# Running sums of the log decay from a high and a low part in the rounded format

## The chip, the cores and the metric

The kernel runs on one core of one Trainium2 chip. The metric is the device time of one execution in microseconds (us). One execution was also taken by the hardware profiler. The profile's names for the engines are used throughout: PE is TensorE (PEld its weight loads), DVE is VectorE, ACT is ScalarE, POOL is GpSimd, SP is SyncE, which starts the DMA transfers.

## The reference

The reference is two transformer blocks in a row, each on 256 tokens of width 1024. The change lies in the second block, in its gated linear attention (GLA). There a low-rank gate gives each of 4 heads x 64 key channels a log decay per token, which is summed up along the tokens inside chunks of 64:

```python
def gla(q, k, v, g_lr, og, w_gate2, b_gate, norm_o):
    log_a = jax.nn.log_sigmoid((g_lr @ w_gate2 + b_gate).astype(jnp.float32)) / GLA_GATE_TAU   # 16
    gh = heads(log_a, GLA_HEAD_K)
    bcum = jnp.cumsum(chunks(gh), axis=3)                 # running sum in each chunk of 64 tokens
    ...
    def step(state, xs):
        qc, kc, vc, bc = xs
        o_inter = jnp.einsum('bhcd,bhde->bhce', qc * jnp.exp(bc), state)
        diff = bc[:, :, :, None, :] - bc[:, :, None, :, :]
        decay = jnp.exp(jnp.where(causal[:, :, None], diff, -jnp.inf))
        attn = jnp.einsum('bhid,bhjd,bhijd->bhij', qc, kc, decay)
        ...
        b_last = bc[:, :, -1:, :]
        k_dec = kc * jnp.exp(b_last - bc)                 # needs the sum of what comes after a token
```

The rest of the two blocks is large matrix products: input projections, attention, output projections and a gated feed-forward net in each block.

## The kernel before

**Tiling.** Tokens stand on the 128 partitions in two tiles (`TOKS` = 2). Every large product `x @ W` is done in strips of 128 rows of W (one strip is a *unit*, up to 1024 columns wide). W comes from memory by DMA into `weights_raw`, a ring of nine slots (`RING`). Each strip is then split in two by `advance`, which exists on ACT and on DVE: ACT writes the strip rounded to the format `fp32r` (float32r, the rounded format; `weights_high`, line 724), and DVE writes what the rounding left (`weights_low`, line 1574, `raw - high`). PE makes a product in three passes in the rounded format: high x high, high x low, low x high (line 1193), 128x512 each, all accumulating in the PSUM tile `acc`. The small products of the attention parts go to four other PSUM banks, `aux[0]` to `aux[3]`.

**Order.** Nothing is scheduled at run time. The function `timeline` writes one list of steps, and each engine goes through this same list, doing its own part of each step. A weight split is put in front of the first step whose place in the list has passed the strip's due time (`due`, reckoned from where PE needs the strip), so between two steps of an engine there may be one or more splits. `tick` counts up a semaphore, and `at` gives the value to wait for.

**The place of the change.** The GLA gate runs during the projection `gla_qk` (eight strips of 512 columns, line 1193). Its steps are in `timeline`, lines 267 to 269: `decay_logits` after the strip (1, 2), which means token tile 1, strip 2, and `decay_sums` together with `gla_qk_turn` 0 after the strip (1, 7), the last of this projection.

- `decay_logits`: PE makes the gate's logits (line 1436). DVE adds the bias (line 1955) and makes the absolute value (1957). ACT takes exp and ln (986, 989, each with a load of its table). DVE makes the log decay `gl` ("log_decay" in the trace, 128x512 f32: two token tiles of 256 channels; line 1960) and counts up `vec`.
- `decay_sums`: PE waits for `vec` and for the masks `sum_up_to` and `sum_after`, two constant 128x128 matrices of 0 and 1/16 which POOL has made at line 2178 to 2185. It then makes four plain f32 products of 128x128 (line 1447, to `aux[0]`; the log decay is the stationary operand, so these sums come out with channels on the partitions) and two plain f32 products of 128x256 (line 1450, to `aux[1]`). ACT copies the first (`bT`, "decay_sum_T", line 992) and takes exp of the second (`kdec`, "k_decayed", line 994). Each plain f32 product stands in the trace as two records, so there are 8 and 4.
- `gla_qk_turn`: PE transposes the projection (line 1103, 4 per token tile), and goes on with the next projection, `gla_v_og` (line 1193).
- `gla_decay` and what follows on DVE and ACT (1974, 1976, 1007, 1987) work from `bT`.

```python
                elif kind == "decay_sums":            # PE
                    pe.wait_ge(*at("vec", "log_decay"))
                    pe.wait_ge(*at("pool", "sum_masks"))
```

## Time and profile before

| | us |
|---|---|
| time, median of 3 runs | 745.93 (745.63 to 746.54) |
| the profiled execution, its own time | 745.29 |
| span of the profiled execution, first to last instruction | 743.5 |
| PE busy in it | 736.3 (99%), 4082 matmul records |
| PE weight loads busy | 610.1 (82%) |
| DVE busy | 487.1 (66%) |
| ACT busy | 401.9 (54%) |
| POOL busy | 56.5 (8%) |
| mean granted clock of PE | 0.999 |

A matmul record's duration contains the time that the pipeline needs to empty, and the next matmul starts before it ends. What one more matmul costs a busy PE is therefore the distance from its start to the next start, not its duration. In a timeline row the first number is the start, the second the time from that start to the end of the last of the merged records, and "xN" their number. DVE and ACT instructions overlap by some 0.1 us in the same way.

### The profile page before, as it was taken

Reading aid. Unit: us, or ns where it says so; the run is one execution under the profiler, and the core shown is the slowest. Engines: PE = TensorE matmul, PEld = TensorE weight load, DVE = VectorE, ACT = ScalarE, POOL = GpSimd, SP = SyncE. Lnnn points to the kernel's source line nnn. Section 1 sums busy time; section 2 is a strip of 40 time slices with the busy share of each in tenths; the row PEclk is TensorE's granted clock in tenths of the full one; section 3 lists DMA queues with packets and bytes.
Section 4 is the critical chain, followed back from the end, with each engine's and each line's share of the span. In section 5 each row is a group of like instructions: output and inputs, shape, how many; then the busy total and the mean of one; then the engine's idle time right before and its main releaser. Section 6 shows DMA issues by size and latency. Waiting matters only on the chain.

```text
span 743.5 us, 10597 instructions
## 1 busy us (share of the span) xinstructions
PE 736.3 (99%) x4082; PEld 610.1 (82%) x4082; DVE 487.1 (66%) x748; ACT 401.9 (54%) x584; POOL 56.5 (8%) x127
## 2 busy tenths in 40 slices
PE   9999999999999999999999999999999999999996
PEld 7888887888888888888898888888888888888886
DVE  5597777676864756775376877777755576475733
ACT  5656767533653535544368554786435545364422
POOL 1100100000470000000023000200011000000000
PEclk9999999999999999999999999999999999999999
DMA  8856464564755655645476373444465565565541
GB/s 320 274 186 224 129 202 140 169 208 150 240 174 176 211 179 173 225 148 194 135 228 208 111 244 118 145 159 121 143 222 162 180 215 167 184 215 159 193 142 57
DMA packets 57521, 134.36 MB, mean 181 GB/s; under 512 B 7864, under 2 KB 13823, under 8 KB 57471
## 3 DMA queue, kind: packets, MB, share of 16 engines
q1 hardware_dynamic: 56816, 132.16, 54.6%
q10 hardware_dynamic: 654, 1.53, 0.6%
q8 instruction: 32, 0.52, 0.3%
q14 instruction: 19, 0.15, 0.1%
HBM read 132.61 MB, written 1.05 MB: 180 GB/s over the span
## 4 chain that ended last, share of the span: by engine, by line
PE 98%; DMA 1%; ACT 0%; DVE 0%; POOL 0%; ACTq 0%; issue 0%; POOLq 0%
PE acc L1193 88%; PE aux L1103 2%; PE aux L1384 1%; PE aux L1288 1%; PE aux L1411 1%; PE acc L1184 1%; PE aux L1309 1%; PE aux L1470 1%; DMA weights_raw<-in_w_in_dram 1%; PE aux L1375 0%; PE aux L1329 0%; PE acc L1123 0%; PE aux L1350 0%; PE aux L1531 0%; PE aux L1184 0%; PE aux L1502 0%
## 5 line engine op out<-in xcount | busy, mean ns | idle before, releaser
L1193 PE MATMUL acc<-weights_high,h_high 128*128 128x512 f32 (+1 forms) x716 | 227.2, 393 | 0.0
L1574 DVE SCALAR_TENSOR_TENSOR weights_low<-weights_raw,gain_columns,weights_high 128x1024 fp32r<-128x1024 f32 (+3 forms) x189 | 217.6, 1188 | 13.0 <-ACT weights_high L724 12.9
L1193 PE MATMUL acc<-weights_high,h_low 128*128 128x512 f32 (+1 forms) x716 | 222.7, 387 | 0.0
L1193 PE MATMUL acc<-weights_low,h_high 128*128 128x512 f32 (+1 forms) x716 | 222.5, 386 | 0.0
L724 ACT ACTIVATE weights_high<-weights_raw,gain_columns 128x1024 fp32r<-128x1024 f32 (+3 forms) x188 | 194.8, 1074 | 33.4 <-DMA weights_raw<-in_w_up_dram 12.0
L1193 PEld LDWEIGHTS acc<-weights_low,h_high 128*128 128x128 f32 x716 | 133.5, 188 | 27.8 <-DVE weights_low L1574 0.6
L1193 PEld LDWEIGHTS acc<-weights_high,h_low 128*128 128x128 f32 x716 | 133.6, 188 | 27.2
L1193 PEld LDWEIGHTS acc<-weights_high,h_high 128*128 128x128 f32 x716 | 130.4, 188 | 26.0 <-issue 1.0
L1571 DVE TENSOR_TENSOR weights_low<-weights_raw,weights_high 128x1024 fp32r<-128x1024 f32 x68 | 80.7, 1219 | 33.2 <-ACT weights_high L724 33.1
L724 ACT ACTIVATE weights_high<-weights_raw 128x1024 fp32r<-128x1024 f32 x68 | 69.3, 1057 | 48.2 <-DMA weights_raw<-in_ffn_w_down_dram 22.2
L1701 DVE SCALAR_TENSOR_TENSOR silu_tmp<-silu_tmp,acc 128x512 f32<-128x512 f32 (+1 forms) x24 | 15.4, 642 | 74.9 <-ACT silu_tmp L781 74.9
L781 ACT ACTIVATE silu_tmp<-acc,stats 128x512 f32<-128x512 f32 (+1 forms) x24 | 15.7, 654 | 87.2 <-PE acc L1193 87.2
L2130 POOL TENSOR_SCALAR stats<-stats 128x1 f32<-128x1 f32 (+1 forms) x15 | 6.5, 432 | 595.2 <-ACT row L737 278.2
L1193 PE MATMUL acc<-weights_high,y_high 128*128 128x512 f32 (+1 forms) x148 | 45.7, 390 | 0.0
L1193 PE MATMUL acc<-weights_high,y_low 128*128 128x512 f32 (+1 forms) x148 | 45.0, 385 | 0.0
L1193 PE MATMUL acc<-weights_low,y_high 128*128 128x512 f32 (+1 forms) x148 | 45.0, 385 | 0.0
L1193 PEld LDWEIGHTS acc<-weights_high,y_low 128*128 128x128 f32 x148 | 27.7, 188 | 5.4
L1193 PEld LDWEIGHTS acc<-weights_low,y_high 128*128 128x128 f32 x148 | 27.7, 188 | 5.4
L1193 PE MATMUL acc<-weights_high,f_high 128*128 128x512 f32 x102 | 31.5, 390 | 0.0
L1193 PE MATMUL acc<-weights_low,f_high 128*128 128x512 f32 x102 | 31.4, 389 | 0.0
L1193 PE MATMUL acc<-weights_high,f_low 128*128 128x512 f32 x102 | 31.4, 389 | 0.0
L1193 PEld LDWEIGHTS acc<-weights_high,y_high 128*128 128x128 f32 x148 | 27.1, 188 | 5.2 <-issue 0.3
(313 smaller groups left out, 645.2 us busy)
## 6 DMA issues: line engine op xcount, KB each, us to landing
weights_raw<-in_w_in_dram SPq DMA_DIRECT2D x59, 512.0 KB, 4.7
weights_raw<-in_w_gate_dram SPq DMA_DIRECT2D x44, 256.0 KB, 3.3
weights_raw<-in_w_up_dram SPq DMA_DIRECT2D x44, 256.0 KB, 4.1
weights_raw<-in_w_down_dram SPq DMA_DIRECT2D x22, 512.0 KB, 4.5
weights_raw<-in_ffn_w_gate_dram SPq DMA_DIRECT2D x44, 256.0 KB, 3.4
weights_raw<-in_ffn_w_up_dram SPq DMA_DIRECT2D x44, 256.0 KB, 4.2
weights_raw<-in_ffn_w_down_dram SPq DMA_DIRECT2D x22, 512.0 KB, 4.4
weights_raw<-in_w_out_dram SPq DMA_DIRECT2D x16, 512.0 KB, 4.6
```

Of the source, the lines that this page charges most:

```text
L724: nc.scalar.activation(hi[:, u % RING, d:d + w], raw[:, u % RING, d:d + w], ACT.Copy, scale=1.0 if g is None else gcol[:, g:g + 1])\
L781: nc.scalar.activation(fe[:, j % 2, t, 0:w], a0[:, 0:w], ACT.Tanh, scale=stat(("half", (tag, t))))\
L1103: i = nc.tensor.transpose(aux[bank][0:w, n * P:(n + 1) * P], src, ident[:, :])
L1184: i = nc.tensor.matmul(dst, lhs[:, k0, sl], w[:, u % RING, c], start=(alone and n == 0 and kt == first_half), stop=(kt == kts - 1 and n == 2))
L1193: i = nc.tensor.matmul(acc[:, 2 * t + b, 0:width], lhs[:, k0, sl], w[:, u % RING, base + d:base + d + width], start=(kt == 0 and n == 0), ...
L1288: m = nc.tensor.matmul(scores(kind, i, hb), att_q(kind, hb, i, pq), att_k(kind, hb, i, pk), start=(n == 0), stop=(n == 2))
L1309: m = nc.tensor.matmul(scores(kind, i, hb), att_q(kind, hb, i, pq), att_k(kind, hb, i, pk), start=(n == 0), stop=(n == len(passes) - 1))
L1384: m = nc.tensor.matmul(aux[bank][hb * HD:hb * HD + HD, d:d + P], v[:, kt, c:c + HD], probs_block(kind, i, hb, kt), start=(kt == 0), stop=( ...
L1411: i = nc.tensor.transpose(aux[first + g][:, d:d + ROWS], fe[r, int(name[-1]) % 2, t, k * P:(k + 1) * P], ident[r, r])
L1571: i = nc.vector.tensor_tensor(lo[:, u % RING, c], raw[:, u % RING, c], hi[:, u % RING, c].bitcast(F32), ALU.subtract)
L1574: i = nc.vector.scalar_tensor_tensor(lo[:, u % RING, c], raw[:, u % RING, c], gcol[:, g:g + 1], hi[:, u % RING, c].bitcast(F32), ALU.mult, ...
L1701: then(nc.vector.scalar_tensor_tensor(e, e, 1.0, a0[:, 0:w], ALU.add, ALU.mult))
```

## The change

The sums are made from two operands in the rounded format in place of one plain f32 operand. ACT copies `gl` rounded into `gl_parts[0]` ("log_decay_high"), DVE subtracts that from `gl` into `gl_parts[1]` ("log_decay_low"), and POOL copies the two masks into the rounded format. PE then makes each of the six products in two passes, high and low, which accumulate: eight instructions of 128x128 and four of 128x256. PE's wait for the log decay becomes a wait for its low part. A DVE wait behind the log decay is new as well.

```diff
+        sum_masks = [sb(f"{n}_rounded", [P, P], F32R) for n in ("sum_up_to", "sum_after")]
...
+            gl_parts = [sb(f"log_decay_{part}", [P, TOKS, 256], F32R, s) for part in ("high", "low")]
...
                 elif kind == "decay_sums":                                   # ACT
+                    act.wait_ge(*at("vec", "log_decay"))
+                    nc.scalar.activation(gl_parts[0][:, :, :], gl[:, :, :], ACT.Copy).then_inc(*tick("act", "log_decay_high"))
                     act.wait_ge(*at("gla_done", "sums"))
...
                 elif kind == "decay_sums":                                   # PE
-                    pe.wait_ge(*at("vec", "log_decay"))
+                    pe.wait_ge(*at("vec", "log_decay_low"))
                     pe.wait_ge(*at("pool", "sum_masks"))
...
-                            nc.tensor.matmul(aux[0][:, c:c + P], gl[:, t, f * P:(f + 1) * P], upto[:, :],
-                                             start=True, stop=True)
+                            for n, part in enumerate(gl_parts):
+                                nc.tensor.matmul(aux[0][:, c:c + P], part[:, t, f * P:(f + 1) * P], sum_masks[0][:, :],
+                                                 start=(n == 0), stop=(n == 1))
                     for t in range(TOKS):
-                        m = nc.tensor.matmul(aux[1][:, t * 256:t * 256 + 256], after[:, :], gl[:, t, :],
-                                             start=True, stop=True)
+                        for n, part in enumerate(gl_parts):
+                            m = nc.tensor.matmul(aux[1][:, t * 256:t * 256 + 256], sum_masks[1][:, :], part[:, t, :],
+                                                 start=(n == 0), stop=(n == 1))
...
-                                                          ALU.min, ALU.subtract), "vec", "log_decay")
+                                                          ALU.min, ALU.subtract), "vec", "log_decay", True)
+                elif kind == "decay_sums":                                   # DVE
+                    dve.wait_ge(*at("act", "log_decay_high"))
+                    signal(nc.vector.tensor_tensor(gl_parts[1][:, :, :], gl[:, :, :], gl_parts[0][:, :, :].bitcast(F32),
+                                                   ALU.subtract), "vec", "log_decay_low")
...
-                done(g.memset(after[64:128, 0:64], 0.0), "pool", "sum_masks")
+                then(g.memset(after[64:128, 0:64], 0.0))
+                g.tensor_copy(sum_masks[0][:, :], upto[:, :])
+                done(g.tensor_copy(sum_masks[1][:, :], after[:, :]), "pool", "sum_masks")
```

On DVE these instructions stand in a row around the gate of the GLA before the change (L1960 makes the log decay, L1574 is a weight split, L1974 the first use of the sums):

```order
L1955 TENSOR_TENSOR log_decay<-aux,gla_bias_bc 128x256
L1957 SCALAR_TENSOR_TENSOR level_decay<-log_decay 128x512 [waits vec]
L1960 SCALAR_TENSOR_TENSOR log_decay<-log_decay,level_decay 128x512 [waits act]
L1574 SCALAR_TENSOR_TENSOR weights_low<-weights_raw,gain_columns,weights_high 128x1024 [waits high_ready]
L1574 SCALAR_TENSOR_TENSOR weights_low<-weights_raw,gain_columns,weights_high 128x1024 [waits high_ready,mm_done] x2
L1974 TENSOR_TENSOR level_decay<-decay_sum_T 128x8x32 [waits act]
```

And the same place on DVE in the changed kernel, whose lines are numbered some lines higher (L1580 is the weight split):

```order
L1961 TENSOR_TENSOR log_decay<-aux,gla_bias_bc 128x256
L1963 SCALAR_TENSOR_TENSOR level_decay<-log_decay 128x512 [waits vec]
L1966 SCALAR_TENSOR_TENSOR log_decay<-log_decay,level_decay 128x512 [waits act]
L1580 SCALAR_TENSOR_TENSOR weights_low<-weights_raw,gain_columns,weights_high 128x1024 [waits high_ready,vec]
L1580 SCALAR_TENSOR_TENSOR weights_low<-weights_raw,gain_columns,weights_high 128x1024 [waits high_ready,mm_done]
L1970 TENSOR_TENSOR log_decay_low<-log_decay,log_decay_high 128x512 [waits act]
L1580 SCALAR_TENSOR_TENSOR weights_low<-weights_raw,gain_columns,weights_high 128x1024 [waits high_ready,mm_done]
L1984 TENSOR_TENSOR level_decay<-decay_sum_T 128x8x32 [waits act]
```

The subtraction that makes the low part stands behind two of the three weight splits and ahead of the third.

On ACT the same place before the change (L724 is a weight split, L789 the copy of the projection out of PSUM, L992 the copy of the sums):

```order
L989 ACTIVATE level_decay<-level_decay 128x512 [waits act]
L724 ACTIVATE weights_high<-weights_raw,gain_columns 128x1024 [waits gains,raw_loaded1]
L789 ACTIVATE gla_qk<-acc,stats 128x512 [waits rstd,mm_done]
L724 ACTIVATE weights_high<-weights_raw,gain_columns 128x1024 [waits gains,raw_loaded2]
L992 ACTIVATE decay_sum_T<-aux 128x512 [waits gla_done]
```

And in the changed kernel:

```order
L991 ACTIVATE level_decay<-level_decay 128x512 [waits act]
L726 ACTIVATE weights_high<-weights_raw,gain_columns 128x1024 [waits gains,raw_loaded1]
L791 ACTIVATE gla_qk<-acc,stats 128x512 [waits rstd,mm_done]
L726 ACTIVATE weights_high<-weights_raw,gain_columns 128x1024 [waits gains,raw_loaded2]
L994 ACTIVATE log_decay_high<-log_decay 128x512 [waits vec]
L996 ACTIVATE decay_sum_T<-aux 128x512 [waits gla_done]
```

The rounded copy comes behind both weight splits and directly ahead of the copy of the sums.

## Rows read from the trace of the kernel before

**Rows 1.** The page: busy us, share of the span and instructions of each engine.

```profile
PE 736.3 (99%) x4082; PEld 610.1 (82%) x4082; DVE 487.1 (66%) x748; ACT 401.9 (54%) x584; POOL 56.5 (8%) x127
```

**Rows 2.** Waits of PE, whole span: whom for, us in total, times, longest.

```profile
PE aux L1092 <- DVE row L2090: 1.1, 1, 1.1
PE acc L1123 <- ACT weights_high L712: 0.5, 1, 0.5
```

**Rows 3.** Timeline of PE around the sums: start, us to the end, operation, count.

```profile
402.90 0.39 PE L1193 MATMUL acc<-weights_low,h_high 128*128 128x512 f32 x1
403.13 1.05 PE L1447 MATMUL aux<-sum_up_to,log_decay 128*128 128x128 f32 x8
404.02 1.03 PE L1450 MATMUL aux<-log_decay,sum_after 128*128 128x256 f32 x4
404.89 0.60 PE L1103 MATMUL aux<-ident,gla_qk 128*128 128x128 f32 x4
```

**Rows 4.** Timeline of DVE, 397 to 405 us.

```profile
397.54 0.74 DVE L1955 TENSOR_TENSOR log_decay<-aux,gla_bias_bc 128x256 f32<-128x256 f32 x2
398.32 0.69 DVE L1957 SCALAR_TENSOR_TENSOR level_decay<-log_decay 128x512 f32<-128x512 f32 x1
401.66 0.69 DVE L1960 SCALAR_TENSOR_TENSOR log_decay<-log_decay,level_decay 128x512 f32<-128x512 f32 x1 [2.64 <-ACT level_decay L989]
402.27 3.67 DVE L1574 SCALAR_TENSOR_TENSOR weights_low<-weights_raw,gain_columns,weights_high 128x1024 fp32r<-128x1024 f32 x3
```

**Rows 5.** Timeline of ACT, 401 to 406 us.

```profile
401.53 1.14 ACT L724 ACTIVATE weights_high<-weights_raw,gain_columns 128x1024 fp32r<-128x1024 f32 x1
402.57 0.67 ACT L789 ACTIVATE gla_qk<-acc,stats 128x512 f32<-128x512 f32 x1
403.14 1.14 ACT L724 ACTIVATE weights_high<-weights_raw,gain_columns 128x1024 fp32r<-128x1024 f32 x1
405.09 0.60 ACT L992 ACTIVATE decay_sum_T<-aux 128x512 f32<-128x512 f32 x1 [0.81 <-PE aux L1450]
```

**Rows 6.** Groups by line and form, ACT and DVE: count, busy us, mean ns.

```profile
L1036 ACT ACTIVATE k_latent_high<-k_latent_first 96x512 fp32r<-96x512 f32 x2 | 1.1, 622 | 0.0
...
L2058 DVE TENSOR_TENSOR k_latent_low<-k_latent_first,k_latent_high 96x512 fp32r<-96x512 f32 x2 | 1.3, 679 | 0.0
```

**Rows 7.** Timeline of PE: rounded products at 256 columns near the end (15 in a row).

```profile
737.51 0.28 PE L1184 MATMUL aux<-weights_high,f_low 128*128 128x256 f32 x1
737.63 0.28 PE L1184 MATMUL aux<-weights_low,f_high 128*128 128x256 f32 x1
```

**Rows 8.** Weight loads by group: rounded operand, plain operand, transpose; busy us, mean ns.

```profile
L1184 PEld LDWEIGHTS aux<-weights_high,f_high 128*128 128x128 f32 x5 | 1.0, 192 | 0.0
L1447 PEld LDWEIGHTS aux<-sum_up_to,log_decay 128*128 128x128 f32 x8 | 1.0, 191 | 0.1
L1103 PEld LDWEIGHTS aux<-ident,gla_qk 128*128 128x128 f32 x8 | 1.0, 140 | 0.2
```

**Rows 9.** Timelines of ACT and PE around PE's last wait, at 6 us.

```profile
5.80 0.71 ACT L715 ACTIVATE weights_high<-weights_raw,gain_columns 128x512 fp32r<-128x512 f32 x1
...
6.04 1.02 PE L1123 MATMUL acc<-weights_high,h_high 128*128 128x512 f32 x2 [0.46 <-ACT weights_high L712]
6.90 0.62 PE L1123 MATMUL acc<-weights_high,h_low 128*128 128x512 f32 x2
```

**Rows 10.** Timeline of PE in the first microseconds.

```profile
3.31 1.65 PE L1092 MATMUL aux<-row 128*128 128x128 f32 x6
4.75 0.51 PE L1103 MATMUL aux<-ident,x 128*128 128x128 f32 x2
```

**Rows 11.** Stretches behind PE's last product: busy times, granted clock, DMA share, GB/s.

```profile
737.90:742.20 4.30, 0.01 (x1) 0.00 (x0) 1.81 (x5) 0.62 (x1) 0.60 (x1) 1.00 0.24 92
742.30:743.50 1.20, 0.00 (x0) 0.00 (x0) 0.00 (x0) 0.00 (x0) 0.00 (x0) 0.50 0.23 79
```

**Rows 12.** Timeline of POOL: the last instruction on the two masks.

```profile
204.45 0.15 POOL L2185 MEMSET sum_after<- 64x64 f32 x1
```

## The prediction

> **What bounds the kernel now.** I read the page's engine line first: PE is busy for 736.3 of 743.5 us, DVE for 487.1 and ACT for 401.9 [rows 1]. Next the waits of PE over the whole span. There are two, both in the first microseconds: PE starts 1.1 us late, and the later wait ends at 6.04 us [rows 2, 9]. From there to its last product at 737.63 us [rows 7] PE never waits for another engine. The reader is to see two things in this. Time taken out of PE's row of work is gained one for one, and time put into it, as work or as a wait, is lost one for one, because no later wait exists that could swallow it. And a busy second of DVE or ACT costs nothing as long as PE still finds its operands ready. So the change is decided at one place, where PE passes from the projection to the sums. The timelines of PE, DVE and ACT there are read side by side.
>
> **PE before.** The sums start at 403.13, the next step (transposes) at 404.89 [rows 3]. They fill 1.76 us: eight records of 128x128 from 403.13 to 404.02, 0.111 each, and four of 128x256 from 404.02 to 404.89, 0.217 each. There is no gap ahead of them: the last 128x512 record starts at 402.90, 0.23 earlier. The log decay is only just in time for that, since DVE finishes it at 401.66 + 0.69 = 402.35 [rows 4] and PE loads its first sum's weights at about 402.9.
>
> **PE's work after.** Four instructions of 128x256 in the rounded format. Such products stand in the trace at 0.12 from start to start (737.51, 737.63) [rows 7], so 4 x 0.12 = 0.48 in place of 0.87, a gain of 0.39. The eight of 128x128 in the rounded format have no row. Bounds: per column the rounded product costs half of the plain record (0.12 to 0.217 at 256), and a straight line through 0.23 at 512 columns (402.90 to 403.13) [rows 3] and 0.12 at 256 gives 0.065 at 128, so 0.52 for eight. From above, a rounded product that at 128 columns is as dear as a whole plain one (two records) costs 0.22, so 1.78 for eight. Between them stands the weight load. Each of the eight has its own 128x128 load. It lasts 192 ns for a rounded operand and 191 for a plain one, against 140 for a transpose [rows 8]; so the format takes nothing off the load, and consecutive plain 128x128 records with the same load stand 0.111 apart. What a load costs where no product hides it is worked out below, about 0.11. I take 0.115 for each, 0.92 for eight, which is the row of the plain ones and a little: the nearest row by load and columns. PE's work after is 0.92 + 0.48 = 1.40, a gain of 0.36 (bounds 0.76 gain, 0.50 loss).
>
> The Trainium skill has two rules here that point in opposite ways. "FP8 and Floating Point Precision", section "TensorE Precision Notes", has true FP32 as four passes through the array. By it two passes in place of four halve the sums, 1.76 to an estimated 0.88 us; the trace agrees nearly at 256 columns (0.217 x 2 to 0.12 x 2) and has no row at 128. "TensorE: Matmul & The Clock Gate", section "LDWEIGHTS (loading the stationary operand)", has a load take its columns divided by 1.2 in ns, 107 for 128 columns, however many rows, by which the halving stops at an estimated 8 x 0.107 + 0.48 = 1.34 us; the trace agrees with equal load times for both formats.
>
> **The wait that is put in.** PE now waits for the low part, and that is made by a chain of three on two other engines, each in its own queue.
> - ACT: the copy stands behind the weight split of 403.14 in its queue. Successive starts there are 401.53 and 402.57, so such a split holds the engine for 1.04 [rows 5], and the copy starts at 404.18. The log decay itself is there since 402.35, so the queue and not the data decides. A copy of 512 columns from SBUF to the rounded format takes 0.622 (96 partitions) [rows 6] to 0.71 (L715, with a gain) [rows 9]. It has no gain: 0.62, end at 404.80.
> - DVE: the new wait behind the log decay costs 0.04 (402.35 to 402.39; as 397.54 + 0.74 = 398.28 to 398.32), where the split started at 402.27 before. Two splits of (3.67 - 1.28)/2 = 1.195 each [rows 4], where 1.28 is one split's own duration, stand ahead of the subtraction: 402.39 + 2.39 = 404.78. The copy arrives at 404.80 + 0.04 = 404.84, so the two queues end within 0.06 of one another, and taking one away would leave the other. The subtraction takes 0.68, as L2058 does [rows 6]: end at 405.52.
> - PE: from a release to the next product but one. ACT's second half-strip ends at 5.80 + 0.71 = 6.51, it releases a 128x512 product, and the product behind that starts at 6.90 [rows 9], 0.39 later, where one such product takes 0.23. So release and restart cost 0.16, of which some 0.05 is the semaphore and 0.11 the weight load that nothing hides.
>
> So the sums end at 405.52 + 0.16 + 1.40 = 407.08, where they ended at 404.89: **2.19 us later**. Bounds of the chain: copy 0.60 (L992, from PSUM) [rows 5] to 0.71, subtraction 0.68 to 0.75 (as a split's 1.28 for 1024 columns scaled with a fixed part), so -0.02 to +0.17. As a second way of adding: PE stands still from 403.13 to 405.68 (2.55) and gains 0.36 of work.
>
> **What lies behind.** Nothing gives the 2.19 back, and little adds to it. While PE waits, queued behind it are the four transposes (404.89 [rows 3]) and the strips of `gla_v_og`, whose operands were ready; they just start later. ACT's copy of the sums waits for PE as it did (0.81 before [rows 5]) and moves by the same 2.19, and with it exp and the level steps; all stay in step with PE. Queued behind DVE's subtraction is the third split, pushed from 404.66 to 405.4, ending at 406.7. It is the strip three further on, and PE, being later by 2.19 itself, meets it with more room than before. SP's DMA waits are for strips that PE has used, so they move with PE. On POOL two copies of 128x128 come behind the masks, the last of which is done at 204.60 [rows 12]; the row's instruction takes 0.15 for a quarter of that size, an estimated 0.6 for each copy, over 190 us ahead of their use at 403 us. If that cover were gone they would cost these 1.2 us.
>
> **The sum against the runs.** Span 743.5 + 2.19 = 745.7, and the execution's own 745.29 + 2.19 = 747.48. The three runs have a median of 745.93, 0.64 above that execution, so I forecast the median at 745.93 + 2.19 = 748.1 us, +0.29%. A measurement of this kernel tells about 0.2% (1.5 us) from no change.
>
> **The rivals.**
> - B, the weight load hides: eight rounded products at 0.065 each, 0.52 + 0.48 = 1.00 of work. The sums end at 405.52 + 0.16 + 1.00 = 406.68, +1.79: 747.7. For it: at 256 columns the rounded product does follow its columns. Against it: 190 ns loads. The four-pass rule above would give an estimated +1.67. 0.13.
> - C, a rounded product of 128 columns is as slow as a whole plain one, so the change doesn't make that part cheaper: 1.78 + 0.48 = 2.26 of work, +3.05: 749.0. For it: no row shows a rounded one that narrow. Against: 256 columns run at full pace. 0.06.
> - D, the stall lowers PE's clock. PE does nothing from about 403.3 to 405.6, 2.3 us. In the trace the granted clock stands at full after 4.3 us with no product (737.90 to 742.20) and at 0.50, the lower level of 1.2 GHz, from 742.30 on [rows 11], so a longer stop than this did not lower it until then. The price: at the start PE ran 128x128 records at 0.24 ((4.75 - 3.31)/6 [rows 10]) in place of 0.111 from its first product at 1.1 us [rows 2] to about 4.9, for 3.8 us; as long a spell at half pace loses 1.9 us, +4.1: 750.0. 0.05.
> - E, the other side: the copy and the subtraction come to run in front of the splits, not behind them, so that PE waits for them alone. This needs ACT and DVE to be early by a split: if ACT is through its split when the log decay is there at 402.35, the low part ends at 402.39 + 0.62 + 0.04 + 0.68 = 403.73, the sums at 403.73 + 0.16 + 1.40 = 405.29, +0.4: 746.3, no change to be told. It decides from a low part that is ready by 404.8 on (then +1.5). Against it: both orders are written down, the change's own order has one split on ACT and two on DVE ahead, ACT is busy without a gap from 401.53 to 404.28, and DVE's first split starts as soon as the log decay is out [rows 4, 5]. Even this best case isn't faster, as the log decay is finished only 0.6 before PE needs it. 0.05.
>
> **How the numbers follow.** Chances: the forecast 0.71, B 0.13, C 0.06, D 0.05, E 0.05. Predicted is the forecast's 748.1. The runs before spread from 745.63 to 746.54, 0.3 below and 0.6 above their median, so the forecast's own 747.9 to 748.3 becomes 747.4 to 748.9 as a measured median. With B below and C above, the range is 747.1 to 749.3; it leaves out D, E and some of the rest. Slower by over 0.2% needs +1.5 us: the forecast, B, C and D give it, less one time in twenty-five when the spread eats the margin (B has only 0.3 of it): 0.89. Within 0.2%: E and that remainder, 0.09. Faster by over 0.2% has no mechanism, since even with no wait at all PE gains 0.36 to 0.76 us: 0.02.
>
> **What the changed profile would show.** PE's waits have a new row, the sums waiting for DVE's low part, 2.2 to 2.6 us, once. The high copy starts on ACT right behind a weight split, near 404.2, and the subtraction on DVE behind the second split, near 404.85. Eight rounded records of 128x128 stand 0.11 to 0.12 apart (0.065 for B, 0.22 for C), four of 128x256 0.12 apart. The clock stays at full in that slice (0.5 for D). The span behind the sums is as long as before. The prediction is wrong if PE's wait is under 1.7 us, if a later wait or stretch of PE makes up or adds a microsecond, or if products away from this place change their pace.

## The result, and the profile after

The changed kernel takes 748.97 us (median of six runs) where the kernel before took 746.23 beside it: 1.0036 times as long, 95% interval 1.0025 to 1.0047. Timed twice more, it gave 749.17 against 745.59 (1.0041, 1.0028 to 1.0055) and 749.3 against 745.45 (1.0041, 1.0029 to 1.0053). So the change costs 2.7 to 3.9 us. Forecast were 748.1 us, +2.2, in a range from 747.1 to 749.3. All ratios are of fast executions; the one execution left out by that, of experiment 3, took 4212 us.

The engine line of the changed kernel, answering [rows 1], shows that no engine has got noticeably more work:

```profile
PE 737.7 (99%) x4082; PEld 611.6 (82%) x4082; DVE 488.1 (65%) x749; ACT 401.6 (54%) x585; POOL 57.3 (8%) x129
```

The waits of PE over the whole span (for whom, us in total, times, longest) answer [rows 2]. The two of before are still there, and one is new, with 2.3 us, the wait for the low part:

```profile
PE aux L1452 <- DVE log_decay_low L1970: 2.3, 1, 2.3
PE aux L1096 <- DVE row L2100: 1.1, 1, 1.1
PE acc L1127 <- ACT weights_high L714: 0.4, 1, 0.4
```

PE's timeline around the sums, answering [rows 3] (as in every timeline here, each row has the start, the us to the end, the operation and the count):

```profile
404.40 0.39 PE L1197 MATMUL acc<-weights_low,h_high 128*128 128x512 f32 x1
407.07 0.33 PE L1452 MATMUL aux<-sum_up_to_rounded,log_decay_high 128*128 128x128 f32 x1 [2.28 <-DVE log_decay_low L1970]
407.23 0.28 PE L1452 MATMUL aux<-sum_up_to_rounded,log_decay_low 128*128 128x128 f32 x1
...
408.01 0.34 PE L1456 MATMUL aux<-log_decay_high,sum_after_rounded 128*128 128x256 f32 x1
...
408.54 0.60 PE L1107 MATMUL aux<-ident,gla_qk 128*128 128x128 f32 x4
```

From the last product of the projection to the first transpose it is 404.40 to 408.54, 4.14 us, where it was 402.90 to 404.89, 1.99 [rows 3]. The difference is **2.15 us at this place**; 2.19 was forecast. This distance between two fixed points of the program is the measure by which all kernels below are compared, since it doesn't depend on what happened earlier. The two queues that make the low part, DVE answering [rows 4] and ACT answering [rows 5]:

```profile
403.15 0.69 DVE L1966 SCALAR_TENSOR_TENSOR log_decay<-log_decay,level_decay 128x512 f32<-128x512 f32 x1 [2.64 <-ACT level_decay L991]
403.88 2.48 DVE L1580 SCALAR_TENSOR_TENSOR weights_low<-weights_raw,gain_columns,weights_high 128x1024 fp32r<-128x1024 f32 x2
406.32 0.69 DVE L1970 TENSOR_TENSOR log_decay_low<-log_decay,log_decay_high 128x512 fp32r<-128x512 f32 x1
```

```profile
404.63 1.14 ACT L726 ACTIVATE weights_high<-weights_raw,gain_columns 128x1024 fp32r<-128x1024 f32 x1
405.67 0.62 ACT L994 ACTIVATE log_decay_high<-log_decay 128x512 fp32r<-128x512 f32 x1
```

The log decay is out at 403.15 + 0.69 = 403.84. The copy starts 1.83 later, behind ACT's split, and ends at 406.29. The subtraction starts at 406.32, behind DVE's two splits, which end at 406.36 by the profile (ends of a pipelined engine overlap a little), and ends at 407.01. PE starts 0.06 after that.

The span itself grew more, 743.5 to 747.2. Behind the first transpose nothing changed: 332.72 us to the last product in place of 332.74. The other 1.50 us lie ahead of the sums, and all of them in the first eleven microseconds. PE's start in the changed kernel, answering [rows 9]:

```profile
7.57 1.06 PE L1127 MATMUL acc<-weights_high,h_low 128*128 128x512 f32 x2
...
8.71 1.20 PE L1127 MATMUL acc<-weights_low,h_high 128*128 128x512 f32 x2
9.71 0.76 PE L1127 MATMUL acc<-weights_high,h_high 128*128 128x512 f32 x2
...
11.22 0.62 PE L1197 MATMUL acc<-weights_high,h_high 128*128 128x512 f32 x2
```

The two products from 8.71 take 1.00 us to the next, so 0.50 each, twice the 0.23 of a product at full pace. The pair of 7.57 lasts 1.06, where the same pair lasted 0.62 in the kernel before [rows 9], and the one that stands at 11.22 here stood at 9.71. From that product to the last one ahead of the sums it is 393.19 us before (9.71 to 402.90) and 393.18 after (11.22 to 404.40). So PE reached its full pace some 5 us later in this execution. The trace's record of the granted clock says the same: it begins, at the full level, at 4.99 us in the kernel before and at 9.99 us here. For what lies ahead of a record's begin the views of the profile print 1.00 too, so that 1.00 is no measurement. It is not the change's doing: in the next two profiles of the same kernel, `after_again` and `after_third` below, the record begins at 4.68 and 5.58 us, PE is at full pace by 7.40 and 7.06, and the last product ahead of the sums comes at 403.40 and 403.10. Over all fourteen profiles the record begins at 4.5 to 6.5 us in nine, with that last product at 402.9 to 403.9, and at 9.7 to 11.1 us in five, with it at 404.0 to 405.1. (The rest of the spread there is PE's wait for its first weights, 0.0 to 1.2 us.) One span alone can't decide about 2 us here.

### The profile page after: what moved, and what is told of

Read it like the earlier page. It is cut to its first block, busy times and chain, and to the rows that moved or that the text cites. A ratio compares the mean times of both kernels' runs of the same rounds, so it can differ in the third digit from the quotient of the medians.

```text
span 747.2 us, 10602 instructions
## 1 busy us (share of the span) xinstructions
PE 737.7 (99%) x4082; PEld 611.6 (82%) x4082; DVE 488.1 (65%) x749; ACT 401.6 (54%) x585; POOL 57.3 (8%) x129
## 3 DMA queue, kind: packets, MB, share of 16 engines
q10 hardware_dynamic: 654, 1.53, 0.6%
## 4 chain that ended last, share of the span: by engine, by line
PE 96%; DVE 2%; DMA 1%; ACT 1%; issue 0%; ACTq 0%; POOL 0%; POOLq 0%
PE acc L1197 86%; PE aux L1107 2%; PE aux L1388 1%; PE aux L1292 1%; PE aux L1415 1%; DVE weights_low L1580 1%; PE acc L1188 1%; PE aux L1313 1%; PE acc L1127 1%; PE aux L1476 1%; DMA weights_raw<-in_w_in_dram 1%; PE aux L1379 0%; PE aux L1333 0%; PE aux L1354 0%; PE aux L1537 0%
## 5 line engine op out<-in xcount | busy, mean ns | idle before, releaser
L1580 DVE SCALAR_TENSOR_TENSOR weights_low<-weights_raw,gain_columns,weights_high 128x1024 fp32r<-128x1024 f32 (+3 forms) x189 | 217.8, 1189 | 13.3 <-ACT weights_high L726 13.2
L734 ACT ACTIVATE h_high<-aux 128x512 fp32r<-128x512 f32 (+1 forms) x25 | 13.0, 567 | 36.2 <-PE aux L1107 36.2
```

Of the source, the lines that this page charges most:

```text
L734: nc.scalar.activation(dst[0][:, kt0:kt0 + n, t * P:(t + 1) * P], aux[bank][:, 0:n * P].rearrange("p (k s) -> p k s", k=n), ACT.Copy, scal ...
L1580: i = nc.vector.scalar_tensor_tensor(lo[:, u % RING, c], raw[:, u % RING, c], gcol[:, g:g + 1], hi[:, u % RING, c].bitcast(F32), ALU.mult, ...
```

## The experiments

Each is made from the changed kernel, unless said otherwise, and timed beside the kernel before. "At the place" is the time from the last product ahead of the sums to the first transpose, 1.99 before. A "fall" is a stretch in which the granted clock drops to its lower level.

**1. The changed kernel again.**

> The changed kernel once more, unaltered, to tell what of the 3.6 us between the two profiled spans belongs to the change. In those traces the step from the last product ahead of the sums to the first transpose behind them grew from 1.99 to 4.14 us (+2.15), and the way from there to the last product stayed at 332.7; the other 1.5 us arose in the first 10 us, where the granted clock rose at 5.0 us in one and at 10.0 us in the other. Theory (the place of the sums alone counts, the start is chance): the clock's rise moves about from execution to execution in both kernels, this profile shows again +2.15 at the sums, and the median lies 2.2 us (1.7 to 2.7) above the kernel before. Rival (the change also slows the start, for example by the places of its buffers): the clock rises near 10 us again and again, and the median lies 3.5 us above.

Measured: 749.17 us against 745.59 (above), 3.58 more where at most 2.7 were expected, and 4.20 at the place. The rival is out, since PE reached its full pace early here (above). The wait is 2.28 as in the first profile, but now the span behind the sums is longer too: 334.28 us, 1.54 more than in the kernel before. The busy times by stretch (PE, PEld, DVE, ACT, POOL, then the granted clock, DMA share, GB/s) say where:

```profile
403.00:406.00 3.00, 0.79 (x4) 0.33 (x2) 3.00 (x4) 2.29 (x4) 0.00 (x0) 1.00 0.82 234
406.00:409.00 3.00, 2.93 (x18) 2.84 (x19) 1.74 (x4) 1.14 (x2) 0.00 (x0) 0.74 0.18 72
409.00:412.00 3.00, 3.00 (x11) 2.40 (x10) 0.23 (x1) 2.99 (x6) 0.00 (x0) 0.69 0.00 0
412.00:420.00 8.00, 8.00 (x39) 6.61 (x38) 7.39 (x13) 5.10 (x9) 0.00 (x0) 1.00 0.22 55
```

The clock is full while PE stands still (first row), and at 0.5, which is 1.2 GHz, for 3.4 us of the second and third rows (3 x 0.26 x 2 + 3 x 0.31 x 2 = 3.4). In these 3.4 us PE's products run at half pace:

```profile
407.60 1.05 PE L1107 MATMUL aux<-ident,gla_qk 128*128 128x128 f32 x4
408.31 1.20 PE L1197 MATMUL acc<-weights_high,h_high 128*128 128x512 f32 x2
...
410.96 0.63 PE L1197 MATMUL acc<-weights_high,h_high 128*128 128x512 f32 x2
```

Two products from 408.31 take 1.00, two from 410.96 on 0.46. The wait has thus a second price, paid after it, in some executions and not in others. This was rival D, which the forecast had at 0.05.

**2. The wait alone.** The copy, the subtraction and PE's wait stay, the sums are plain products as before:

```
-  for n, part in enumerate(gl_parts):
-      nc.tensor.matmul(aux[0][:, c:c + P], part[:, t, f * P:(f + 1) * P], sum_masks[0][:, :], start=(n == 0), stop=(n == 1))
+  nc.tensor.matmul(aux[0][:, c:c + P], gl[:, t, f * P:(f + 1) * P], upto[:, :], start=True, stop=True)
   ... (the same for aux[1], with after and gl)
```

> The copies, the subtraction and PE's wait for the low part stay, but PE makes the plain f32 products of the kernel before. Theory (two terms, a wait of 2.3 and a gain of 0.36 on PE): PE waits 2.3 us as in the changed kernel, the step from the last product ahead of the sums to the first transpose takes 4.14 + 0.4 = 4.5 us, and the time is 2.5 us over the kernel before. Rival (the gain on PE is nothing, since the weight loads set the pace of all of them): 4.14 again, 2.15 over the kernel before.

```profile
403.11 0.39 PE L1197 MATMUL acc<-weights_low,h_high 128*128 128x512 f32 x1
405.78 1.16 PE L1451 MATMUL aux<-sum_up_to,log_decay 128*128 128x128 f32 x8 [2.28 <-DVE log_decay_low L1968]
406.77 1.03 PE L1454 MATMUL aux<-log_decay,sum_after 128*128 128x256 f32 x4
407.64 0.60 PE L1107 MATMUL aux<-ident,gla_qk 128*128 128x128 f32 x4
```

Measured: 403.11 to 407.64 is 4.53 at the place, 2.54 more than before, and 748.08 us against 745.59 (+2.49; 1.0032, 1.002 to 1.0044). The wait is the same 2.28. The rounded passes therefore give back 4.53 - 4.14 = 0.39 us, and the wait costs the rest.

**3. The passes alone.** DVE writes the log decay in the rounded format at once, both passes read it, and the copy and the subtraction are gone; the low part is thereby left out and the high one summed twice:

```
-  act.wait_ge(*at("vec", "log_decay"))
-  nc.scalar.activation(gl_parts[0][:, :, :], gl[:, :, :], ACT.Copy).then_inc(*tick("act", "log_decay_high"))
   ...
-  for n, part in enumerate(gl_parts):                          # in both kinds of sums
+  for n, part in enumerate((gl_parts[0], gl_parts[0])):
   ...
-  pe.wait_ge(*at("vec", "log_decay_low"))
+  pe.wait_ge(*at("vec", "log_decay"))
   ...
-  signal(nc.vector.scalar_tensor_tensor(gl[:, :, :], ..., ALU.min, ALU.subtract), "vec", "log_decay", True)
-  (the subtraction of L1970)
+  signal(nc.vector.scalar_tensor_tensor(gl_parts[0][:, :, :], ..., ALU.min, ALU.subtract), "vec", "log_decay")
```

> No wait is put in: DVE writes the log decay itself in the rounded format, there is no copy, no subtraction and no DVE wait, and PE makes both passes from this one operand (so the low part is left out and the sums are doubled). Theory: PE doesn't wait, eight records stand 0.111 apart and four 0.12, the step from the last product ahead of the sums to the first transpose takes 1.99 - 0.39 = 1.6 us, and the time is 0.4 us under the kernel before, within the noise. Rival (the narrow rounded products follow their columns once no stall is ahead of them): 0.065 apart, 1.2 us, 0.8 under.

```profile
403.36 0.39 PE L1195 MATMUL acc<-weights_low,h_high 128*128 128x512 f32 x1
403.58 1.00 PE L1450 MATMUL aux<-sum_up_to_rounded,log_decay_high 128*128 128x128 f32 x8
404.43 0.69 PE L1454 MATMUL aux<-log_decay_high,sum_after_rounded 128*128 128x256 f32 x4
404.95 0.60 PE L1105 MATMUL aux<-ident,gla_qk 128*128 128x128 f32 x4
```

Measured: 1.59 at the place, 0.40 less than before, no wait; 745.13 us against 745.59 (0.9992, 0.9983 to 1.0). Read it row by row against [rows 3]: eight narrow ones from 403.58 to 404.43, 0.85, where the plain ones took 0.89; four wide ones from 404.43 to 404.95, 0.52 for 0.87. Nearly all the gain is in the wide ones. This kernel can't be used, but it says what the two passes give when nothing has to be waited for: 0.4 us, 0.05% of the time.

**4. What sets the narrow products' pace.** As experiment 3, but the stationary operand of the eight has 64 columns in place of 128 (the sums up to the token of half of the channels are left out, and ACT fills their place from the log decay). The rows and columns that stream through are as many as before:

```
-  nc.tensor.matmul(aux[0][:, c:c + P], part[:, t, f * P:(f + 1) * P], sum_masks[0][:, :],
+  nc.tensor.matmul(aux[0][0:64, c:c + P], part[:, t, f * P:f * P + 64], sum_masks[0][:, :],
```

> The kernel with the passes alone and no wait, in which the eight products of the first kind take only 64 of their 128 stationary columns, so that each weight load is half as long and the moving operand keeps its 128 columns (the sums of half the channels are left out, and ACT fills their place with the log decay in one more copy). Theory (the weight load sets the pace of a rounded product of 128 columns): the eight stand 0.055 to 0.07 us apart in place of 0.11. Rival (the pace is the array's own for 128 moving columns in this format): 0.11 apart as before.

PE's timeline, and the weight loads of the eight as a group (busy us, mean ns), ahead of them those of experiment 3:

```profile
404.77 0.64 PE L1451 MATMUL aux<-sum_up_to_rounded,log_decay_high 128*64 128x128 f32 x8
405.25 0.69 PE L1455 MATMUL aux<-log_decay_high,sum_after_rounded 128*128 128x256 f32 x4
```

```profile
L1450 PEld LDWEIGHTS aux<-sum_up_to_rounded,log_decay_high 128*128 128x128 f32 x8 | 1.0, 191 | 0.1
```

```profile
L1451 PEld LDWEIGHTS aux<-sum_up_to_rounded,log_decay_high 128*64 128x64 f32 x8 | 0.6, 134 | 0.1
```

Measured: the eight take 0.48 us, 0.060 each, in place of 0.106 (0.85 / 8) in experiment 3. Halving the load alone nearly halves them, with the same stream of 128 columns. So the weight load sets the pace of a rounded product of 128 columns. By its stream alone such a product takes 0.06 or less, about rival B's 0.065; only the load keeps it from it. The first two of the eight show this at full width too. Where the sums follow 512-column products without a wait, the load of the second isn't held up by a load close ahead of it: in experiment 3 the first two loads start 0.23 apart, the others 0.11. There the second product comes 0.06 after the first, and the others 0.11 apart. `sums_later` (experiment 7) has the same:

```profile
408.59 0.22 PE L1453 MATMUL aux<-sum_up_to_rounded,log_decay_high 128*128 128x128 f32 x1
408.64 0.28 PE L1453 MATMUL aux<-sum_up_to_rounded,log_decay_low 128*128 128x128 f32 x1
408.76 0.27 PE L1453 MATMUL aux<-sum_up_to_rounded,log_decay_high 128*128 128x128 f32 x1
```

The plain records don't behave so: in the trace of the kernel before, the first of the eight is followed after 0.108, the others after 0.111. Their stream alone is thus about as long as the load takes (half of the 0.217 at 256 columns is 0.108 as well). So the rounded format does halve the stream at 128 columns, and gains nothing by it, because the load then takes over at the same 0.11.

**5. Both ahead of the splits.** The copy and the subtraction are queued straight behind the operation that makes the log decay, on ACT and on DVE:

```
                     nc.scalar.activation(gz[:, :, :], gz[:, :, :], ACT.Ln, bias=1.0)...
-                elif kind == "decay_sums":
                     act.wait_ge(*at("vec", "log_decay"))
                     nc.scalar.activation(gl_parts[0][:, :, :], gl[:, :, :], ACT.Copy)...
+                elif kind == "decay_sums":
                     act.wait_ge(*at("gla_done", "sums"))
   ... (on DVE)
                     signal(nc.vector.scalar_tensor_tensor(gl[:, :, :], ...), "vec", "log_decay", True)
-                elif kind == "decay_sums":
                     dve.wait_ge(*at("act", "log_decay_high"))
```

> The copy on ACT and the subtraction on DVE stand directly behind the log decay, ahead of the weight splits; nothing is left out. Theory (the wait is mostly the queue ahead of the two): the low part is ready 1.38 us behind the log decay, PE waits about 0.7 us, the step around the sums takes 2.4 us, and the time is 0.4 us over the kernel before. Rival (the splits that are pushed back come too late for PE, which then waits there): the wait moves to the strips of the next projection, and the time stays 1.5 us or more over.

PE and DVE:

```profile
404.98 0.33 PE L1452 MATMUL aux<-sum_up_to_rounded,log_decay_high 128*128 128x128 f32 x1 [0.57 <-DVE log_decay_low L1969]
...
406.45 0.60 PE L1107 MATMUL aux<-ident,gla_qk 128*128 128x128 f32 x4
```

```profile
404.23 0.69 DVE L1969 TENSOR_TENSOR log_decay_low<-log_decay,log_decay_high 128x512 fp32r<-128x512 f32 x1 [0.77 <-ACT log_decay_high L993]
```

Measured: 2.43 at the place (404.02 to 406.45), 0.44 more than before, and 746.05 us against 745.59 (+0.46; 1.0005, 0.9997 to 1.0014). This is rival E's case with its price (+0.4). The queues' order, not the two operations, makes four fifths of the loss.

**6. One of the two ahead.** Only ACT's half of experiment 5 in `act_first`, only DVE's half in `dve_first`.

> Of the two moves ahead of the weight splits only that of the copy on ACT; the subtraction on DVE stays behind two splits. Theory (both queues end within 0.06 us of one another, so taking one away leaves the other): the step from the last product ahead of the sums to the first transpose takes 4.1 us where the changed kernel has 4.15, and PE waits 2.2 us. Rival (ACT's queue is what counts): PE waits under 1.5 us.

> Only the subtraction moves ahead of the weight splits on DVE, where it now waits for the copy, which stays behind the split on ACT. Theory (the same tie): PE waits 2.3 us as in the changed kernel, the step takes 4.15 us; DVE stands idle for 2.5 us ahead of the subtraction and makes all three splits behind it, which nobody waits for. Rival (DVE's queue is what counts): PE waits under 1.5 us; or the late splits make PE wait again at the next projection's strips, and the time is a further microsecond up.

For `dve_first` 4.21 at the place (403.86 to 408.07) and 749.41 us against 745.67 (1.0045, 1.0031 to 1.0059): the same as the changed kernel, as both theories had it for a tie of the two queues. `act_first` came out at 4.98 (403.00 to 407.98), 0.84 *worse* than the changed kernel, where a tie would have left it alone; 749.98 us (1.0063, 1.0048 to 1.0079). Of that 0.54 is the wait, 2.82 in place of 2.28. The other 0.3 is a fall that begins inside the sums, at 407.29: from there on the wide products stand 0.21 or 0.22 apart. Its PE, ACT and DVE show this and what was missed:

```profile
406.20 0.33 PE L1452 MATMUL aux<-sum_up_to_rounded,log_decay_high 128*128 128x128 f32 x1 [2.82 <-DVE log_decay_low L1970]
```

```profile
402.48 0.63 ACT L993 ACTIVATE log_decay_high<-log_decay 128x512 fp32r<-128x512 f32 x1 [0.76 <-DVE log_decay L1966]
```

```profile
404.26 1.28 DVE L1580 SCALAR_TENSOR_TENSOR weights_low<-weights_raw,gain_columns,weights_high 128x1024 fp32r<-128x1024 f32 x1 [0.50 <-ACT weights_high L726]
405.46 0.69 DVE L1970 TENSOR_TENSOR log_decay_low<-log_decay,log_decay_high 128x512 fp32r<-128x512 f32 x1
```

ACT waits 0.76 for the log decay with its next split queued behind it. DVE's second split needs that split's high part, and waits 0.50 for it; the subtraction stands behind that split. The copy, moved ahead on one engine, thus delayed the subtraction on the other.

**7. The sums later.** The step is cut in two: the copy and the subtraction stay at (1, 7). The products move behind the transposes and behind the first twelve products of the next projection.

```
-                           (1, 7): [do("decay_sums"), do("gla_qk_turn", 0)]})
+                           (1, 7): [do("decay_parts"), do("gla_qk_turn", 0)]})
-    g[0] = [do("gla_decay", 0)]
+    g[0] = [do("decay_sums"), do("gla_decay", 0)]
```

In `first_and_later` the copy and the subtraction are queued as in experiment 5 besides.

> Nothing is left out. The copy on ACT and the subtraction on DVE stay where the change put them, but PE, and the readers of the sums, take their step two strips of the next projection later (2.7 us of PE's work further on, behind the transposes). Theory (the loss is PE's waiting, and work that PE has at hand covers it): PE doesn't wait at the sums, the clock never falls, PE gains 0.36 us, and the time is 0.4 us under the kernel before, within the noise. Rival (the level steps that start from the sums have no room, so a later start makes PE wait at the level products near 421 us): a new wait of PE of up to 1 us at these products, and the time is up to 0.6 over the kernel before.

> Nothing is left out. Copy and subtraction directly behind the log decay, ahead of the weight splits, and PE's step two strips later. Theory: no wait, as with the later step alone, 0.4 us under the kernel before; and the sums' readers start on ACT somewhat earlier than with the later step alone. Rival (the pushed-back splits come late for the two strips that PE now takes first): PE waits for a low part of the weights at 405 to 409 us, and the time is over the kernel before.

PE's waits and timeline in `sums_later`, with ACT's copy that the transposes need:

```profile
PE aux L1097 <- DVE row L2101: 1.1, 1, 1.1
PE acc L1128 <- ACT weights_high L714: 0.5, 1, 0.5
```

```profile
404.95 0.39 PE L1198 MATMUL acc<-weights_low,h_high 128*128 128x512 f32 x1
405.33 0.65 PE L1108 MATMUL aux<-ident,gla_qk 128*128 128x128 f32 x4
...
409.96 0.64 PE L1198 MATMUL acc<-weights_high,h_high 128*128 128x512 f32 x2
```

```profile
404.61 0.67 ACT L791 ACTIVATE gla_qk<-acc,stats 128x512 f32<-128x512 f32 x1
```

The wait is gone from PE's list. From the last product ahead of the transposes to the first product behind the sums it is 5.01 us (404.95 to 409.96); the same two products stand 5.19 apart before (402.90 to 408.09). Measured 745.70 us against 745.67 (1.0, 0.9992 to 1.0009): the whole loss is back, and 0.18 at the place on top, too little to be told from nothing in the time. Of the 0.36 to 0.40 that the passes gain, some 0.15 is lost again because PE now comes to the transposes before ACT's copy of `gla_qk` (404.61 + 0.67 = 405.28) lets it go on, and 0.06 because after this short stop they take 0.41 to the next product in place of 0.35.

`first_and_later` is the worse of the two: 746.79 us (1.0016, 1.0007 to 1.0025), +1.12. The copy of the log decay ahead in ACT's queue pushes ACT's copy of `gla_qk`, and PE waits for that at the transposes:

```profile
404.82 0.66 PE L1107 MATMUL aux<-ident,gla_qk 128*128 128x128 f32 x4 [1.38 <-ACT gla_qk L791]
```

So what helped with the sums in their old place hurts with the sums moved.

**8. A longer wait.** Is it the length of the stop that decides about the clock? Five more copies of the log decay, each waiting for the one before it, are put behind the copy on ACT.

```
+  for k in range(5):
+      nc.scalar.activation(gl_parts[0][:, :, :], gl[:, :, :], ACT.Copy).then_inc(*tick("act", ("copy", k)))
+      act.wait_ge(*at("act", ("copy", k)))
```

Beside it the changed kernel and experiment 2 were timed again.

> The copy on ACT is made six times, one behind the other, and only the last is waited for, which makes PE's wait longer by 5 x 0.67 = 3.3 us, 5.6 in all. Nothing is left out. Theory (a longer stall lowers the clock every time): every run at 0.996 or less, the time is 2.15 + 3.3 + 1.5 = 7 us over the kernel before. Rival (a stall costs its own length only): 5.5 over.

> The changed kernel once more, to count. In 12 of its runs so far the mean granted clock was 0.996 or less in 6, and the one of these with a trace shows the clock at 1.2 GHz for 3.4 us from 1.3 us behind PE's stall on, which cost 1.5 us. Theory (the stall sometimes lowers the clock): about half of the runs again have 0.996 or less and lie 1 to 1.5 us above the others, whose lower end is 747.5 to 748. Rival (the drop was chance of another chip state): none here.

> The plain products of the kernel before behind the changed kernel's wait, once more, to count drops of the clock: none in 5 runs so far. Theory (what follows the stall decides as well as the stall: eight rounded 128x128 products keep the array half as busy as plain ones at the same pace): again none or one run at 0.996 or less, median 2.5 us over the kernel before. Rival (the stall alone decides, and 5 runs were luck): about half of the runs, as in the changed kernel, median 3.3 over.

```profile
402.93 0.39 PE L1201 MATMUL acc<-weights_low,h_high 128*128 128x512 f32 x1
408.94 0.48 PE L1456 MATMUL aux<-sum_up_to_rounded,log_decay_high 128*128 128x128 f32 x1 [5.62 <-DVE log_decay_low L1974]
409.21 0.42 PE L1456 MATMUL aux<-sum_up_to_rounded,log_decay_low 128*128 128x128 f32 x1
...
411.67 1.05 PE L1111 MATMUL aux<-ident,gla_qk 128*128 128x128 f32 x4
```

Measured: 8.74 at the place, of which 5.62 is waiting, with the sums already at half pace; the granted clock stands at 0.5 from 408.54 to 415.36, 6.8 us. 753.95 us against 745.45: +8.5, which is 6.75 at the place and 1.7 behind it. Expected were 7: the wait came out as said (3.34 longer), but the sums themselves took 2.73 in place of 1.47, at half pace. `after_third` has 4.14 at the place and no fall in its profile (749.3 against 745.45), `wait_only_again` 4.54 and none in its profile, yet 749.83 us (1.0058, 1.0041 to 1.0074), 1.9 more above its kernel before than in experiment 2, where 2.5 were expected by the one theory and 3.3 by the other.

The fall leaves its mark in the mean granted clock of an execution too. 3.4 us at half take 0.002 off the mean (1.7 / 748). The four profiles with a fall have means of 0.994 to 0.996, the ten without 0.998 to 1.000. The mark isn't sharp, because the stretch at 0.5 at the end of the program [rows 11] counts in the mean as well. It is 0.4 to 3.6 us long in the profiles and takes up to 0.002 off by itself. So 0.997 can be either and isn't counted as a fall below. There is one such execution of the plain sums, with 752.79 us the slowest of them, and one of the kernel before. Counted that way over all executions, by the length of PE's wait:

| kernels | PE's wait | executions with a fall |
|---|---|---|
| before; passes_only, sums_later | none | none |
| both_first | 0.6 us | 0 of 11 |
| first_and_later | 1.4 us, elsewhere | 0 of 11 |
| changed kernel with plain sums (experiment 2, both timings) | 2.3 us | 2 of 11, or 3 |
| changed kernel | 2.3 us | 8 of 17 |
| dve_first | 2.35 us | 1 of 4 |
| act_first | 2.8 us | 4 of 4 |
| long_stall | 5.6 us | 4 of 4 |

With the length the falls become the rule; only five lengths were tried. In the changed kernel the eight executions with one have a mean of 749.44 us, the nine without 748.45. The profiles put the price of a fall of 3.4 us at 1.6 us: all of it behind the sums in `after_again` and `dve_first`, 1.3 there and 0.3 in the sums in `act_first`.

## Why the prediction was right, and where it was thin

**The bound.** That a time put into PE's row of work is lost one for one held: `wait_only` lost 2.54 at the place and 2.49 in the median, `both_first` 0.44 and 0.46, `passes_only` gained 0.40 and 0.46, and nothing behind the sums gave anything back (332.72 to 332.80 us in every profile without a fall where the transposes follow the sums; 332.74 before).

**PE's work.** Forecast 1.40 us, measured 407.07 to 408.54, 1.47, with a part of the restart in it that the forecast counted apart (the second product comes 0.16 after the first, the next ones 0.11 apart). From the end of the subtraction to the transposes it is 1.56 by the forecast and 1.53 measured. The narrow products stand 0.11 apart (0.115 forecast), the wide ones 0.12 but for the first, 0.17 or 0.18. The gain against plain products was put at 0.36 and is 0.39. The choice in this step was between two rules of the Trainium skill. At 256 columns the halving holds: 0.217 to 0.12. At 128 it doesn't hold: 0.111 to 0.106 or 0.11. Experiment 4 gives the reason, by which the step rests on a run and not only on equal load times: with half the load, 0.06. The Trainium skill's rule that bears here is that of "TensorE: Matmul & The Clock Gate", section "LDWEIGHTS (loading the stationary operand)", columns divided by 1.2, an estimated 107 ns for 128 columns and 53 for 64; the runs have 106 to 111 and 60. The four passes of the Trainium skill's "FP8 and Floating Point Precision", section "TensorE Precision Notes", are borne out by the stream alone, which halves (0.108 to some 0.06, experiment 4). At 128 columns the load of 0.11 hides it.

**The wait.** Every link was within 0.05: the copy starts 1.83 after the log decay is out (forecast 1.83), takes 0.62 (0.62), the subtraction starts 2.48 after it (2.49) and takes 0.69 (0.68), PE waits 2.28 (2.2 to 2.6). That the two queues tie was right as a reading of the changed kernel, and `dve_first` bears it out. Its corollary, "taking one away would leave the other", was incomplete: on ACT's side taking one away lengthens the wait by another 0.54, by the high part that DVE's split waits for (experiment 6).

**What lies behind.** Right in the profiles without a fall. Of the small terms, POOL's two copies took 0.29 each in place of 0.6, some 200 us ahead of their use, and cost nothing.

**Rival D, the clock.** This is the step that failed, though the forecast time is near. It argued that the clock "stands at full after 4.3 us with no product", so that "a longer stop than this did not lower it until then". In experiment 1 the clock fell 1.4 us *after* PE had resumed (406.07 to 407.46), not in the stop. The row at the end of the program [rows 11] shows a stop with no work behind it; it says when the record changes and not what a stop does to the work that follows. The rival was also put as all or nothing with 1.9 us; in truth it comes in some half of the executions, at 1.6 each. By the count above that adds 8/17 x 1.6 = 0.75 to the mean, and 2.15 + 0.75 = 2.9 is what the changed kernel should lie above the one before on average. The means of the three timings differ by 2.54, 3.36 and 3.05 us, 2.98 over all 17 executions. The medians differ by 2.74, 3.58 and 3.85; a median doesn't add up in this way. The forecast's 2.19 is below all of these: the mechanism was right and its local size exact, but the total lacked this term.

**The range.** The first median, 748.97, lies just above the forecast's own band, which ended at 748.9; 749.17 and 749.3 lie further above. The range held the time since it went up to 749.3 for rival C's sake, and C is refuted. That it held was luck. The bands don't come out of their own terms either: 747.9 less 0.3 is 747.6 and not 747.4, and B and C with the same spread would give 747.4 to 749.6 and not 747.1 to 749.3.

**What stays open.** What decides whether a 2.3 us stop is followed by a fall isn't known. Of the eight profiles with a stop of 2.3 us or more, the two with a late start have no fall, and of the six with an early one four have. So the executions without a fall hold more of the late starts, which may be why the two groups' means lie only 0.99 apart and not 1.6. Whether what PE does behind the stop matters (2 or 3 of 11 with plain sums against 8 of 17 with rounded ones at the same 2.28 us) isn't settled by these counts. That `wait_only` came to +2.5 in one timing and to +4.4 in the other is explained for the profiled executions alone. In the first, PE's last product ahead of the sums comes at 403.11, in the second at 405.06, after a full pace from 10.6 us on and a wait of 1.2 for its first weights. The second thus comes to the place 2.16 later than the kernel before (402.90) and loses 2.54 there, together 4.70 of the 4.73 that it lies above the profiled execution of the kernel before. Two or three of the other five executions of the second timing had a fall. With one profile for each timing the shares can't be told for the rest.

## What to carry to other kernels

A cheaper form of a product is worth what its operand's preparation leaves of it. Here 0.4 us of passes were bought with two operations on two other engines, each queued behind weight splits, and a 2.3 us stop of the bounding engine. Ask of each added operation what stands ahead of it in its queue at that moment, and what on the other engine waits for the work that it pushes back. If the preparation can't come straight behind its data, let the consumer come later (the sums behind the transposes and twelve products cost nothing). And at 128 columns or fewer with a load for each product, look at the load before counting passes. A stop of the tensor engine of two to three microseconds was dearer here than it was long: count its length, and some 1.6 us for a lowered clock in part of the executions.

## What the runs showed of the hardware

- After a stop of 2.3 us the granted clock of the tensor engine fell to 0.5, in 8 of 17 executions of the changed kernel by their mean clock, for 3.4 us in the one with a profile; after 2.8 and 5.6 us in 8 of 8, in the profile of the latter for 6.8 us; after 0.6 us in 0 of 11. In the profiles with 2.3 to 2.8 us of stop it fell 1.1 to 1.9 us after the engine had resumed, in the one with 5.6 us 0.4 ahead of that. A stop's own stretch with the clock at 1.00 says nothing about what follows.
- At the start PE ran at half pace until 4.5 to 6.5 us in nine profiles and until 9.7 to 11.1 in five, of kernels that do the same there. The record of the granted clock begins then; the 1.00 that the views print for the time ahead of it is no measurement. A late start moves everything behind it by up to 2 us.
- A rounded product of 128x128 takes 0.106 to 0.111 us with a load of 128 columns and 0.060 with one of 64, with the same stream. Where the next load isn't held up by one close ahead, at the first of the eight, it takes 0.05 to 0.06 at full width, and a plain record 0.108.
